# Selection of query tiles 1 and 2 moved into the query units of a two-layer sparse-attention decoder

## The reference

```python
q, k, v, ga, qi, wi, ki, ub, gb, uc, gc = project(rms_norm(x), w_in)   # one input projection
# branch A, prompt: for every query
sc  = sum_h wi[h] * relu(qi[h] . ki / sqrt(32)) / sqrt(8)   # indexer, 8 heads
sc  = where(key_pos <= q_pos, sc, -inf)
idx = top_k(sc, 132)                                        # 132 keys per query
o   = softmax(q . k[idx] / 8) @ v[idx]                     # 8 heads of 64
# branch B: causal pooling; branch C: causal depthwise conv, 31 taps, layer norm, swish
y = concat(A * silu(ga), B * silu(gb), C * silu(gc)) @ w_out;  x = x + y
```

## Time and profile before

| | |
|---|---|
| median of 3 runs | 804.91 us (803.55 to 807.04) |
| the profiled execution | 805.13 us, its span 803.8 us |
| mean granted TensorE clock | 0.958 |
| PE, DVE, ACT, POOL busy | 90%, 68%, 41%, 34% of the span |

### The profile page before, as it was taken

The page is one execution under the profiler, slowest core; times in us unless marked ns, Lnnn a source line. Parts: engine busy times, 40 slices in busy tenths (PEclk is TensorE's granted clock), DMA queues, the critical chain, the costliest instruction groups (busy, mean ns, idle before and its releaser), DMA issues. The chain is left out here.

```text
span 803.8 us, 13109 instructions
## 1 busy us (share of the span) xinstructions
PE 726.5 (90%) x4628; PEld 592.1 (74%) x4628; DVE 547.8 (68%) x1342; ACT 326.1 (41%) x840; POOL 274.4 (34%) x305
## 2 busy tenths in 40 slices
PE   4899999997879798999998999999888789899998
PEld 4896656586768786778998765657776687777888
DVE  3538896799987976435443889669999698632332
ACT  3716445444753342233131554643383624222202
POOL 1012978722744410111110468782174443000000
PEclk8999999999799999999999999999998899899999
DMA  5533040324022535014034304030412135401312
GB/s 181 162 114 108 18 144 2 107 68 137 15 93 80 153 131 180 1 53 148 15 95 123 110 4 145 15 105 32 133 57 80 49 116 181 158 1 33 95 31 107
DMA packets 54977, 71.87 MB, mean 89 GB/s; under 512 B 12977, under 2 KB 30585, under 8 KB 54881
## 3 DMA queue, kind: packets, MB, share of 16 engines
q1 hardware_dynamic: 54802, 70.96, 28.3%
q10 hardware_dynamic: 111, 0.08, 0.0%
HBM read 64.05 MB, written 7.61 MB: 89 GB/s over the span
## 5 line engine op out<-in xcount | busy, mean ns | idle before, releaser
L1187 PE MATMUL R<-x_hi,W_r 128*128 128x268 f32 x448 | 140.4, 313 | 12.1 <-DVE bufA L1530 4.1
L1189 PE MATMUL R<-x_hi,W_r 128*128 128x268 f32 x448 | 134.9, 301 | 0.0
L1188 PE MATMUL R<-x_lo,W_r 128*128 128x268 f32 x448 | 134.7, 301 | 0.0
L1200 PE MATMUL R<-yT,W 128*128 128x268 f32 (+2 forms) x768 | 128.9, 325 | 3.8 <-DVE yT L1530 3.7
L1171 PE MATMUL R<-W_r,x_hi 128*128 128x512 f32 (+3 forms) x320 | 123.4, 386 | 6.5 <-DVE W_r L1530 6.4
L1200 PEld LDWEIGHTS R<-yT,W 128*128 128x128 f32 x768 | 110.4, 195 | 20.7 <-issue 6.7
L1172 PE MATMUL R<-W_r,x_hi 128*128 128x512 f32 (+3 forms) x320 | 119.0, 372 | 0.0
L1173 PE MATMUL R<-W_r,x_lo 128*128 128x512 f32 (+3 forms) x320 | 118.5, 370 | 0.0
L1187 PEld LDWEIGHTS R<-x_hi,W_r 128*128 128x128 f32 x448 | 91.5, 204 | 23.1 <-issue 11.6
L787 POOL TENSOR_TENSOR W_r<-W,W_r 128x1024 fp32r<-128x1024 f32 x28 | 67.0, 2403 | 98.2 <-ACT W_r L896 98.0
L1188 PEld LDWEIGHTS R<-x_lo,W_r 128*128 128x128 f32 x448 | 91.8, 205 | 0.5 <-issue 0.5
(11 more groups left out here) (250 smaller groups left out, 1270.1 us busy)
## 6 DMA issues: line engine op xcount, KB each, us to landing
W<-in_w_in SPq DMA_DIRECT2D x52, 512.0 KB, 4.8
KV<-in_cache_k SPq DMA_DIRECT2D x32, 256.0 KB, 2.8
W<-in_w_out SPq DMA_DIRECT2D x8, 1024.0 KB, 7.2
KV<-in_cache_v SPq DMA_DIRECT2D x32, 256.0 KB, 4.1
ubx<-qkv_rows SPq DMA_DIRECT2D x16, 256.0 KB, 4.3
W<-in_w_in SPq DMA_DIRECT2D x8, 296.0 KB, 3.4
out_new_k_prompt<-kz SPq DMA_DIRECT2D x8, 256.0 KB, 2.1
out_new_v_prompt<-V SPq DMA_DIRECT2D x8, 256.0 KB
```

The costliest lines, as they stand in the source:

```text
L1187: pe.matmul(out, hi[:, cols], x_hi[:, kc, toks], start=(kc == 0), stop=False)
L1188: pe.matmul(out, hi[:, cols], x_lo[:, kc, toks], start=False, stop=False)
L1189: m = pe.matmul(out, lo[:, cols], x_hi[:, kc, toks], start=False, stop=(kc == KC - 1))
L1200: m = pe.matmul(R[:, k, 0:hi - lo], W[:, slot(x), kc % 4, 128 * (u[1] % 4):128 * (u[1] % 4) + 128], yT[:, kc, lo:hi], start=(kc == 0), sto ...
```

## The change

It does three things. Inside the query units, behind each pair of pieces with its taps (behind `kq_sum` where the unit ends), `between(2)` runs two selection steps of tiles 1 and 2: tile 1 and tile 2 in turn until tile 1 has its 7, tile 2 alone from then on. That is 20 steps per layer: 7 of tile 1 and 13 of tile 2. The two `select(1)`, `select(2)` pairs in the conv work become `between(2)` too, four steps of tile 2. The loop then runs until tile 2 has 32 steps, tile 3 28, and tile 4 6, where tile 4 starts when tile 2 has its 32. `late(n)` isn't changed; since a tile that is done issues nothing more, it issues the steps of tile 2 in n = 0 and 1 alone (before: 0, 1 and 2) and those of tile 4 up to n = 19 (before: 22). The number of selection steps per layer is the same.

```diff
-EARLY_STEPS, EARLY_REST = 28, 5
+EARLY_TO, EARLY_REST = {1: 2 * LOW_ROUNDS + 3, 2: 32, 3: 28, 4: 6}, 5
...
+            def between(count):
+
+                for _ in range(count):
+                    select(1 if steps_of[1] < EARLY_TO[1] and steps_of[1] <= steps_of[2] else 2)
+
...
                     for _ in range(TAPS_Q[i] // 2 if x else (TAPS_Q[i] + 1) // 2):
                         tap(j)
                         j += 1
-                kq_sum(NT + i)
+                    if x:
+                        kq_sum(NT + i)
+                    between(2)
             rest(18)
             rest(19)
...
-            select(1)
-            select(2)
+            between(2)
...
-            select(1)
-            select(2)
+            between(2)
...
-            for _ in range(EARLY_STEPS):
-                select(1)
-                select(2)
-                select(3)
+            while any(steps_of[i] < EARLY_TO[i] for i in EARLY_TO):
+                for i in EARLY_TO:
+                    if steps_of[i] < EARLY_TO[i] and (i < 4 or steps_of[2] == EARLY_TO[2]):
+                        select(i)
```

## The result

The changed kernel takes 792.64 us (median of 4, 788.23 to 794.65) against 804.38 us (4 runs, 803.55 to 807.04) for the kernel before: ratio 0.9842, 95% interval 0.9812 to 0.9873, so 1.6% faster. The forecast was 790.7, 785 to 799. The profiled execution took 788.23 us, its span 786.9, its mean clock 0.976 (before: 0.958).

A forecast was written before the change was run, and what follows sets the result against it. PE, busy for 90% of the span, was taken as the bound, its largest wait 20.5 us for DVE's masked copy. Gains of 3.2 + 4.0 = 7.2 us per layer, 14.4 in both, took 805.1 to 790.7 us, range 785 to 799.

The forecast's parts named there:

- Query units, hidden: Query units: about 7 us of added DVE steps per layer, nine of ten places costing nothing inside 11.0 us idle.
- Rival (b): Query units hide nothing: each of ten places holds up PE, +7 us per layer, 805 us, no change; chance 0.11.
- (d): Tile 1's negation, cut and triangle meet POOL in the query units: PE loses 4.2 us per layer, 799; chance 0.04.
- The tenth place: Behind the query units' last gather: two steps make PE 0.6 us late through the value units, bounds 0 to 2.
- The tail and step 2: Ahead of the scores: DVE's first L1881 0.4 us earlier; step 2 loses tile 2's 2.2 us cut and 0.2 us triangle.
- Step 5: Score step 5: tile 3's cut comes before POOL's next instruction, -0.5 us, and PE's 0.84 us wait goes.
- the opening: Score steps 1 to 5: gain 2.4 + 0.8 = 3.2 us per layer, bounds 1.5 to 4.5.
- Steps 19 to 22: Late score steps: waits of 2.12 and 0.98 us go, plus clock; gain 4.0 us per layer, bounds 1.5 to 5.
- The sum: Whole kernel: 3.2 + 4.0 = 7.2 us per layer, 14.4 in both, giving 790.7 us.
- (a): Only one of the gains, 3.2 or 4.0 us per layer, reaches the end: 797 to 799 us; chance 0.13.
- (c): A 1.8 us wait in the first value unit drops PE's clock to 1.2 GHz there: slower, up to 854; chance 0.05.
- (e): Clock stays up in both stretches, `swish` passes ahead of POOL twice: 9 to 10 us per layer, 785 to 787; chance 0.12.

The follow-up runs named there:

- e9: e7 with its last three selection steps put behind the rest of the projections and W_r's cast; 785.1 us, 0.9751 of the kernel before.
- e5: Changed kernel with the query units' last pair of selection steps put behind the rest of the projections and W_r's cast; 790.4 us, 0.9807 of the kernel before.
- e4: Changed kernel with tile 2 taken to 30 steps, so its cut falls in step 2 again, tile 4's six kept; 792.8 us, 0.9836 of the kernel before.
- e12: e9 with one POOL product (rest of W's slot 23) moved behind its wait for the take of unit ub(1,1); 785.8 us, 0.9765 of the kernel before.
- e2: Changed kernel with query-unit selection kept, but 30 steps of tile 2 and none of tile 4 ahead of the scores; 799.5 us, 0.9902 of the kernel before.
- e3: Changed kernel without selection in the query units, keeping tile 2's 32 and tile 4's 6 steps ahead of the scores; 799.8 us, 0.9923 of the kernel before.
- e7: Changed kernel with three selection steps instead of two behind each pair of pieces in the query units; 786.3 us, 0.9771 of the kernel before.
- e10: e9 with 26 instead of 28 of tile 3's steps ahead of the scores; 785.7 us, 0.9759 of the kernel before.
- e11: e7 with none of tile 4's steps ahead of the scores; 799.1 us, 0.9922 of the kernel before.
- e8: Changed kernel with 12 instead of 6 steps of tile 4 ahead of the scores; 799.7 us, 0.9932 of the kernel before.

## Why the prediction was right, step by step

**Query units, hidden: right.** PE is busy for 45.97 us in either window, and from the mark to the value units, less the wait for the cast, PE takes 68.01 us in both. In e9, with half as much again in the places, it takes 68.47. Rival (b) needed 7 us a layer; (d) met 1.07 us once (the triangle of tile 1 at 140.96), under the gap of 1.55 us that was there. One sentence was wrong in part: tile 1's cut and triangle had POOL idle before, its negation did not (0.49 us at 158.06 beside POOL's L833, 0.23 in its new place).

**The tenth place: mis-sized.** The 0.6 us were worked out as two steps and a chain less the 0.25 us of idle time. Step 0 came 1.6 later. By the clock of before the cast started 0.55 us later, as forecast; what the sum lacked is that it took 0.99 longer, since the pair stands between the instruction that releases POOL's products and the cast, which so runs beside both. e5 undoes it and gets the 1.6 back. It lay inside the bounds of 0 to 2.

**The tail and step 2: right.** First L1886 at 187.87, 187.35 with the offset taken off: 0.13 ahead of 187.48, for a forecast of 0.4 and bounds that held it. Two sizes were off against each other: the tail began 1.5 us late and not 0.6, and was 1.7 shorter and not 1.0, 0.97 of it by the product behind the cast, which no longer met POOL. The wait ahead of step 2 fell to 0.79 where 1.5 was named, because PE was later. Ahead of step 4 it is gone, and step 4 starts at 197.4 by the clock of before, for 197.5 forecast. The cut lasts 0.29 us in its new place and 2.24 in the old one (e4).

**Step 5: the step that failed.** "The 0.84 wait at step 5 goes": it became 2.50. I had let tile 3's cut pass ahead of the second L787 and not asked what comes behind it; the triangle did. PE is 2.5 us earlier at step 4 and only 1.5 at step 5's unit, where 3.2 were forecast. The lower bound of 1.5 named such a collision; the opening's gain, from step 0 to 18 less the late start, came out just under it: 2.82 - 1.56 = 1.3 us a layer instead of 3.2. e12 shows the cause, and also that removing it alone is worth nothing yet.

**Step 10: not in the prediction.** It placed the waits at steps 2, 4, 5, 22 and 24. PE waited ahead of step 10 too, 1.46 us in layer 0 and 2.68 in layer 1, the longest of the 13. In the changed kernel these are 2.23 and 2.04, 4.3 of the 7.0 us that are left, and in every other run there is such a wait of 0.8 to 2.7 us in each layer. Right behind it a DVE product of 64x30 elements, 0.17 to 0.20 us in its other places, lasts 5.20 us (217.03) beside two POOL products in a row; the kernel before has the same at 4.87. No experiment moved either, so what they are worth stays open.

**Steps 19 to 22: right, a little low.** 4.8 us for 4.0, with the waits of 2.12 and 0.98 down to 0.35 and none, and the granted clock of steps 18 to 24 up from 0.94 to 1.00. `swish` did pass between the products, by 3.8 us in two pairs; the cut and triangle gave 2.05 of it back at 253.86. The queue of page products did not hold it back.

**The sum.** 6.1 for 7.2 a layer: two errors of opposite sign, -1.9 in the opening and +0.8 behind. That the total came within 2 us of the forecast is so in part luck. The Trainium skill's "VectorE: DVE Perf Modes", section "The DRAIN you can't avoid", would have had the chained steps for nothing; the lone steps of tile 3 in the tail come 1.30 us a pair (184.11 to 185.40), for 1.03 between others, so the row's 0.1 a step or somewhat more stands.

**Rivals.** (a) is refuted by e2 and e3, whose gains add up. (c): the value units of the changed kernel kept a granted 1.00 with waits of 1.77 and 1.56 us in them; in e7, with a wait of 3.17, they fell to 0.95, so the mechanism may be there, further on and small; no run tested it alone. (e) did not come by itself; e7 and e9 reach it.

e9, at 785.1 us, beats both kernels: 2.5% under the kernel before and 0.9% under the changed one by the two ratios. e7, e10 and e12 can't be told from it. Still open is what e12 would be worth with the product held 5 us behind step 10 and L1904 moved out of POOL's way too; that was not tried.

## What to carry to other kernels

A queue that is too long is shortened by moving work into idle time that another engine's latency leaves, and the price is to be sought at the last place, where what follows is no longer a wait but work. When DVE gets earlier, list the POOL instructions of the next 10 us and, for each, which DVE instruction with two SBUF inputs (or a `tensor_scalar` like the cut) will now stand beside it: here a 0.3 us instruction cost what was left of POOL's. Moving one such pair apart is worth little until its successors are placed too, and steps taken ahead pay only up to the wait they empty (six of tile 4: 12.8 us, e7 against e11; twelve: 7 us lost, e8).

## What the runs showed of the hardware

In these traces an instruction of DVE was held for all that was left of POOL's or not at all, by its kind and operands. The triangle (two SBUF inputs) took 2.11, 2.05 (e7) and 1.45 us beside POOL tensor_tensors and 0.26 to 0.28 otherwise, and in the two traces shown ended 0.15 us behind POOL's instruction. MAX8 and MATCH_REPLACE8 of 532 columns kept 0.70 and 0.68 to 0.70 beside the same products, and the product with one input in PSUM (`cc<-R,cc`, 536 columns) 0.71 beside a page sum. In the Trainium skill, "SBUF — State Buffer", section "Who interferes with whom", DVE with two SBUF inputs contends with a GpSimd instruction that reads SBUF, and the one that is second waits for the whole of the other; these traces agree. By that section of the Trainium skill a `tensor_scalar` is held only in a two-port mode. The cut was held (2.24 us at 276 columns), and it does 532 columns in 0.43 us where a MAX8 takes 0.70, so it may run in such a mode; no run here decides that.

A DVE instruction that waits is not next in line either. In the changed kernel the 64x30 product began at 217.03, with POOL's L866 still running (216.51 to 217.51), and ended at 222.23, just behind the two L787 products that POOL ran from 217.49 to 222.18. In the fourteen traces such a product takes 4.9 to 5.2 us in each layer.

POOL's long product pays nothing: the L787 beside the held triangle took 2.36 us, and in e12, with the triangle out of its way, 2.36 as well. Its short instructions can pay: beside the four instructions of the cast in e7, L803 and L804 took 0.79 and 0.77 us, for 0.45 and 0.32 with DVE elsewhere.
